# Inverse's last level on one quarter, keys' norms from a diagonal, and four loads moved, in a retention, delta-rule and PEER block

## What is computed

```python
k_g = k_g * lax.rsqrt(jnp.sum(k_g * k_g, axis=-1, keepdims=True) + NORM_EPS)
kkt = jnp.einsum('bhnid,bhnjd->bhnij', kb, k) * lmask      # kb = k * beta
m = jnp.eye(CHUNK) + jnp.where(strict, kkt, 0.0)
sol = lax.linalg.triangular_solve(m, rhs, left_side=True, lower=True, unit_diagonal=True)
...
act = jax.nn.gelu(jnp.einsum('tkd,td->tk', u_tab[ids], xb), approximate=False)
return jnp.einsum('tk,tkd->td', gate * act, v_tab[ids])
```

## Time and profile before

| | before |
|---|---|
| median of 3 runs | 3143.29 us (3141.07 to 3143.57) |
| the profiled execution | 3143.25 us, of which 3141.3 us are the span of its trace |
| busy PE, DVE, ACT, POOL | 76%, 66%, 37%, 37% of the span |
| moved by the DMA engines | 1265.78 MB, mean 403 GB/s |
| of it by the gathers | 1073.81 MB |
| mean granted TensorE clock | 0.878 |

### The profile page before, as it was taken

One profiled execution on the slowest core, in us unless ns is written; L12 is line 12 of the kernel. 1 busy time (PEld: TensorE's weight loads), 2 busy tenths in 40 slices (PEclk: granted clock), 3 DMA queues, 4 the chain that ended last, 5 costly groups with the idle time before them and its releaser, 6 DMA issues.

```text
span 3141.3 us, 36341 instructions
## 1 busy us (share of the span) xinstructions
PE 2386.6 (76%) x12496; PEld 1389.6 (44%) x12496; DVE 2076.6 (66%) x5408; ACT 1173.6 (37%) x3421; POOL 1175.5 (37%) x1030
## 2 busy tenths in 40 slices
PE   8877787998874787997876587798787567765554
PEld 7753355764541345663552144575355124431111
DVE  4475855668579854667749874656856976486444
ACT  2233433344334432435323533424433343232222
POOL 0033533235333442334434443234443444344442
PEclk9998898998987898998998789899998689877777
DMA  8399999999999999999999999999999999999997
GB/s 344 141 405 420 417 411 401 396 409 419 420 415 400 419 420 420 386 418 419 419 420 415 420 419 416 390 405 420 419 420 420 420 419 418 419 402 418 420 420 319
DMA packets 177736, 1265.78 MB, mean 403 GB/s; under 512 B 21520, under 2 KB 21776, under 8 KB 25104
## 3 DMA queue, kind: packets, MB, share of 16 engines
q0 software_dynamic: 147456, 1073.81, 83.0%
q1 hardware_dynamic: 28368, 183.72, 14.2%
q10 hardware_dynamic: 1728, 5.94, 0.5%
HBM read 1259.19 MB, written 4.19 MB: 402 GB/s over the span
## 4 chain that ended last, share of the span: by engine, by line
DMA 36%; PE 36%; DVE 16%; ACT 6%; issue 3%; POOL 3%; SPq 0%; ACTq 0%; POOLq 0%; DVEq 0%
DMA uv<-uv_tab,ids 33%; PE y_ps L476 13%; PE bank L533 8%; DVE uv L1161 7%; PE bank L525 7%; PE bank L540 3%; POOL uv L452 3%; DMA wbuf<-w 2%; ACT diag L847 2%; PE y_ps L555 1%; DVE area L1221 1%; DVE area L1455 1%; PE bank L590 1%; DMA uv<-w 1%; ACT gelu L841 1%
## 5 line engine op out<-in xcount | busy, mean ns | idle before, releaser
L452 POOL DMA_INDIRECT uv<-uv_tab,ids x1024 | 1175.0, 1147 | 1933.0 <-PE y_ps L476 1589.8
L1161 DVE CUSTOM_DVE_ANT_0 uv<-uv,h 128x1024 f32<-128x1024 f32 x1024 | 1237.6, 1223 | 783.9 <-DMA uv<-uv_tab,ids 777.4
L476 PE MATMUL y_ps<-uv,diag 128*64 128x512 f32 x4096 | 1187.2, 712 | 515.2 <-ACT diag L847 494.1
L476 PEld LDWEIGHTS y_ps<-uv,diag 128*64 128x64 f32 x4096 | 289.1, 156 | 1168.5 <-ACT diag L847 687.4
L841 ACT ACTIVATE gelu<-dots 128x2 f32<-128x2 f32 x512 | 104.1, 203 | 1429.8 <-DVE dots L1161 1429.4
L533 PE MATMUL bank<-actT,wbuf 128*128 128x128 f32 x2688 | 343.0, 289 | 42.8 <-DMA wbuf<-w 37.8
L533 PEld LDWEIGHTS bank<-actT,wbuf 128*128 128x128 f32 x2688 | 329.6, 204 | 99.8 <-issue 72.4
L847 ACT ACTIVATE diag<-gated,gelu 128x64 f32<-128x64 f32 x1024 | 300.7, 340 | 66.9 <-PE y_ps L476 8.2
L837 ACT ACTIVATE gated<-smalls,gate 128x64 f32<-128x64 f32 x1024 | 293.9, 336 | 7.8 <-DVE acc L1175 7.8
L525 PE MATMUL bank<-wbuf,actT 128*128 128x256 f32 x960 | 226.8, 390 | 23.3 <-DMA wbuf<-w 21.5
L525 PEld LDWEIGHTS bank<-wbuf,actT 128*128 128x128 f32 x960 | 181.7, 194 | 91.7 <-issue 49.5
(11 more groups left out here) (221 smaller groups left out, 1874.2 us busy)
## 6 DMA issues: line engine op xcount, KB each, us to landing
wbuf<-w SPq DMA_DIRECT2D x146, 1024.0 KB, 9.5
uv<-w SPq DMA_DIRECT2D x20, 1024.0 KB, 23.9
uv<-uv_tab,ids POOLq DMA_INDIRECT x1024, 16.1
acc<-x SPq DMA_DIRECT2D x8, 512.0 KB, 12.8
y<-acc ACTq DMA_DIRECT2D x8, 512.0 KB, 7.6
rowbuf<-x SPq DMA_DIRECT2D x5, 512.0 KB, 12.6
actT_ahead<-x SPq DMA_DIRECT2D x3, 512.0 KB, 19.1
keys_sb<-keysT ACTq DMA_DIRECT2D x1, 1024.0 KB, 16.0
```

What stands on the lines that cost most here:

```text
L452: nc.gpsimd.indirect_dma_start(out=uv[i % RING][:, :, :].rearrange("p z d -> p (z d)"), out_offset=None, in_=uv_tab, in_offset=bass.Indire ...
L476: done = mm(y_ps[z][64 * j:64 * j + 64, :], diag[:, i % DIAGS, :], uv[i % RING][:, 1, 512 * z:512 * z + 512], start=(s % PAIRS == 0), stop ...
L1161: V.tensor_tensor_reduce(out=u, in0=u, in1=h2[n % 2][:, j, :], scale=1.0, scalar=0.0, op0=ALU.mult, op1=ALU.add, accum_out=dots[:, i % DOT ...
```

## The change

Three edits.

1. **Last level.** At level 6 only the lower left 64x64 quarter of P is non-zero after the mask. The change makes that quarter alone for each head (K=64, 64 columns of weights, 64 columns moved), copies it without a mask, leaves Q and the update of `T` out, and makes and subtracts only the upper right quarter of R.
2. **Keys' norms.** `kk` is made from the unscaled keys, before `ss`. DVE multiplies it with the identity and sums along the rows (`tensor_tensor_reduce`, once a head; its product goes to `NT`, which is written again later), which gives the keys' sums of squares in `st[:, 88:92]`; event `kk_sums`. ACT squares q alone, PE's `ss` has 4 matmuls for 8. `beta_row` now scales `cmask` into `kbT`, and `NT` = `kk` times `kbT`. PE's wait for `kbT` is gone; ACT waits for `kk_sums`. The order of the banks changes with it.
3. **Late loads.** The four loads are issued on ACT after the third projection of chunk 0 has been taken in, at the end of its `inputs`.

```diff
-    uses += own(("gc", "gc_in", 1, 0), ("gc_row", "E", 1, 0), ("ss", "norm_in", 1, 0),
-                ("kT", "kst", 1, 0), ("qk", "attn", 1, 0), ("beta_row", "kbT", 1, 0),
-                ("vT", "vb", 1, 0), ("kk", "NT", 1, 0),
+    uses += own(("gc", "gc_in", 1, 0), ("gc_row", "E", 1, 0), ("kk", "NT", 1, 0), ("ss", "norm_in", 1, 0),
+                ("kT", "kst", 1, 0), ("qk", "attn", 1, 0), ("beta_row", "NT", 1, 0),
+                ("vT", "vb", 1, 0),
...
 # PE, mix
+                pe.wait_ge(*event("silu_conv", n, 0))
+                by_head(n, "kk", conv[:, 4:8, :], conv[:, 4:8, :])
                 pe.wait_ge(*event("sq", n))
                 b = take(n, "ss")
-                for i in range(2 * H):
+                for i in range(H):
...
-                pe.wait_ge(*event("kbT", n))
-                by_head(n, "kk", conv[:, 4:8, :], kbT)
...
+                    if i == LEVELS - 1:
+                        b = take(n, f"P{i}")
+                        for h in range(H):
+                            last = mm(b[64:128, P * h:P * h + 64], NT[0:64, h, 64:128], T[0:64, h, 0:64], start=True, stop=True)
+                        given(last)
+                        turn()
+                        pe.wait_ge(*event("inv_P", n, i - 1))
+                        pe.wait_ge(*event("inv_TT", n, i - 1))
+                        b = take(n, f"R{i}")
+                        for h in range(H):
+                            last = mm(b[0:64, P * h + 64:P * h + 128], Pm[64:128, h, 0:64], TT[64:128, h, 64:128],
+                                      start=True, stop=True)
+                        given(last)
+                        turn()
+                        continue
...
 # ACT: the same four act.dma_start(dst, src) leave the place before act.wait_ge(const_in, ...)
                 if c.kind == "start":
+                    for dst, src in ((ret_qdec[:, :, :], qdec), (smalls[:, :], small),
+                                     (keys_sb[:, :, :], keysT), (lnf_row[:, :], rows.partition_broadcast(P))):
+                        act.dma_start(dst, src).then_inc(late_in, 16)
                     return
...
 # ACT, roots and squares
-                    A(st[:, root][:, H:2 * H], b[:, H:2 * H], ACT.Sqrt, bias=eps_col[:, 0:1]).then_inc(S["norm_in"], 1)
+                    act.wait_ge(*event("kk_sums", n))
+                    A(st[:, root][:, H:2 * H], st[:, 88:92], ACT.Sqrt, bias=eps_col[:, 0:1]).then_inc(S["norm_in"], 1)
...
-                A(norms[:, :, :], conv[:, 0:8, :], ACT.Square).then_inc(S["sq"], 1)
+                A(norms[:, 0:4, :], conv[:, 0:4, :], ACT.Square).then_inc(S["sq"], 1)
...
 # DVE, at the end of log_decays
+                    b = filled(dve, "kk", c)
+                    for h in range(H):
+                        last = V.tensor_tensor_reduce(out=NT[:, h, :], in0=b[:, P * h:P * h + P], in1=ident, scale=1.0, scalar=0.0,
+                                                      op0=ALU.mult, op1=ALU.add, accum_out=st[:, 88 + h:89 + h])
+                    last.then_inc(S["kk_sums"], 1)
...
-                V.tensor_tensor(kbT[:, :, :], conv[:, 4:8, :], heads(filled(dve, "beta_row", c)), ALU.mult
-                                ).then_inc(S["kbT"], 1)
+                link(V.tensor_tensor(kbT[:, :, :], cmask[:, :, :], heads(filled(dve, "beta_row", c)), ALU.mult))
...
-                V.tensor_tensor(NT[:, :, :], heads(filled(dve, "kk", c)), cmask[:, :, :], ALU.mult).then_inc(S["NT"], 1)
+                V.tensor_tensor(NT[:, :, :], heads(filled(dve, "kk", c)), kbT[:, :, :], ALU.mult).then_inc(S["NT"], 1)
...
+                i = LEVELS - 1
+                V.tensor_copy(Pm[64:128, :, 0:64], heads(filled(dve, f"P{i}", c))[64:128, :, 0:64]).then_inc(S["inv_P"], 1)
+                turn()
+                corner = TT[0:64, :, 64:128]
+                V.tensor_tensor(corner, corner, heads(filled(dve, f"R{i}", c))[0:64, :, 64:128], ALU.subtract
+                                ).then_inc(S["inv_TT"], 1)
```

More of the change, by code:

```diff
@@ L74, in level @@
             steps = {level + 1: names for level, names in steps.items()}
-        return (own((f"P{i}", "inv_P", LEVELS - 1, i - 1)) + steps.get(i, [])
-                + own((f"Q{i}", "inv_T", LEVELS - 1, i - 1), (f"R{i}", "inv_TT", LEVELS, i)))
+        made = own((f"P{i}", "inv_P", LEVELS - 1, i - 1)) + steps.get(i, [])
+        if i < LEVELS - 1:
+            made += own((f"Q{i}", "inv_T", LEVELS - 2, i - 1))
+        return made + own((f"R{i}", "inv_TT", LEVELS, i))
     both = int(kind == "start")
@@ L295, in build @@
         picked = scores.rearrange("p a (b t) -> p (a b) t", t=TOPK)
-        st = sb("st", [88])
+        st = sb("st", [92])
         rstd2 = st[:, 85:86]
@@ L325, in build @@
             "ret_mixed": 1, "conv_done": 3, "silu_conv": 3, "sq": 1, "beta_k": 1, "sp_in": 1, "exp_ab": 1,
-            "ln_ab": 1, "beta_g": 1, "diff": 1, "exp_diff": 1, "small_exp": 1, "kst_scale": 1, "qd": 1,
+            "ln_ab": 1, "beta_g": 1, "diff": 1, "kk_sums": 1, "exp_diff": 1, "small_exp": 1, "kst_scale": 1, "qd": 1,
             "kbe": 1, "T_init": 1, "gdn_ss": 1, "sqrt_gdn": 1, "mixed": 1, "ss2": 1, "sqrt2": 1, "rstd2": 1,
@@ L912, in inputs @@
                 if n == 0:
-                    for dst, src in ((ret_qdec[:, :, :], qdec), (smalls[:, :], small),
-                                     (keys_sb[:, :, :], keysT), (lnf_row[:, :], rows.partition_broadcast(P))):
-                        act.dma_start(dst, src).then_inc(late_in, 16)
                     act.wait_ge(const_in, 16 * N_CONST)
@@ L1359, in mix @@
                 turn()
-                for i in range(1, LEVELS):
+                for i in range(1, LEVELS - 1):
                     V.tensor_tensor(Pm[:, :, :], heads(filled(dve, f"P{i}", c)), each_head(level_mask[i]), ALU.mult
```

## The result

| | before, beside it | after |
|---|---|---|
| median | 3143.43 us (4 runs, 3141.07 to 3148.46) | 3096.03 us (4 runs, 3095.97 to 3096.13) |
| span of the profiled execution | 3141.3 us | 3094.0 us |
| first gather starts | 136.4 us | 133.05 us |
| mean granted TensorE clock | 0.878 | 0.879 |

The ratio is 0.9847, with a 95% interval of 0.9835 to 0.9859. The kernel became 47.4 us faster, where 2.4 were forecast, and lies far outside the range. The sign was right, the size was not: something acts here that the forecast doesn't have.

What follows compares the result with a forecast made beforehand. It took a serial program, mostly on PE, to bound the kernel up to some 137 us, then the stream's bytes at 420 GB/s. Terms 0.6 + 1.75 = 2.35 us off 3143.25 gave 3140.9 us, range 3136.0 to 3145.5.

Steps and rivals of the forecast that it cites:

- which is this kernel's ceiling: In the stream: most slices move 415 to 420 GB/s, none more, so that was taken as this kernel's highest rate.
- The stream behind it is bound by bytes and shifts as it is: After the first gather: the whole stream was to start and end 2.35 us earlier, otherwise unchanged.
- The bytes are the same in both kernels: Whole traffic, 1265.78 MB: unchanged, so edits were summed on chunk 0's chain, then their effect on the stream was asked.
- The keys' norms: Chunk 0's chain through DVE: 0.6 us gained, bounds 1.4 gained and 2.9 lost; `T` copied at 55.7 us.
- The last level: PE in chunk 0, level 6: P and R at 0.46 us each, saving 1.75 us, bounds 1.5 and 2.2.
- The late loads: ACT in chunk 0: third projection ends 1.4 us earlier, eaten by 2.25 us of issues; keys' SiLU 0.4 us later.
- Late loads too late: Rival at DVE near 58 us: DVE waits for the loads until 65, 6.1 us lost, 3147.0 us; chance 0.07.
- A dry stream in each mix: Rival: the sums ahead of ACT's roots delay the stream in all seven mixes, 9.8 us lost, 3150.7 us; chance 0.05.
- Lulls shrink: Rival after 145 us: PE's lighter mix removes a fifth of the stream's 48 us shortfall, 3131 us; chance 0.13.
- Head start only in part: Rival on chunk 0's chain: only the last level counts, 3141.5 us, or 3144.4 with costlier sums; chance 0.15.
- the case that I held likeliest: Whole kernel: the forecast's own case, 3140.9 us, 3138 to 3143.5 with the lulls' shifts; chance 0.60.

Runs made afterwards that it cites:

- e8: The kernel before with 32 unused bytes ahead of `wbuf`, so weight buffers stay unaligned while gather buffers start at a multiple of 512; 3102.37 us, ratio 0.9879.
- e13: e1 with 32 bytes between `uv4` and `uv5`, so five gather buffers are aligned and five are 32 bytes off; 3117.03 us, ratio 0.9913.
- e2: The changed kernel with the keys' sums in spare columns of `smalls` and `st` at 88 columns, so addresses stay as before; 3141.67 us, ratio 0.9995.
- e1: The kernel before with `st` at 92 columns for 88, nothing else changed, so gather buffers start at a multiple of 512; 3098.35 us, ratio 0.9860.
- e11: e1 plus the quarter-sized last level alone; 3100.69 us, ratio 0.9867.
- e9: e1 plus the move of the four late loads alone; 3101.60 us, ratio 0.9865.
- e14: The changed kernel with the four late loads issued where they were before the change; 3097.69 us, ratio 0.9854.
- e3: The kernel before with `st` at 100 columns, so gather buffers start 32 bytes past a multiple of 512; 3143.20 us, ratio 1.0000.

## Why the prediction was wrong

**The step that failed is "which is this kernel's ceiling"**, and with it "The stream behind it is bound by bytes and shifts as it is". The rows showed a rate that the slices reach and don't pass. I read a rate that was reached as one that nothing in the kernel sets. The stream was bound by its transfers, as I said, but the time of a transfer's packets depended on where they landed: 312.0 ns in the mean for 317.0, 427 GB/s for 420, 45 us. "The bytes are the same in both kernels" was true and beside the point: 1.4% of the time hung on where they land. The diff held the cause in plain sight. The sums go to `st[:, 88:92]`, so `st` grew by 16 bytes, and I costed its instructions and never asked what lies behind it. No rival had a changed packet, so the range couldn't hold the result either.

The trace of before held a hint that I didn't use, packets of one size at 309, 313 and 320 ns. Nothing in my account gave equal packets different times; the question why they had them could have led to their addresses. The Trainium skill, "DMA: Bandwidth & Descriptors", section "How a descriptor splits into AXI transactions", says of reading that a transaction must start at a multiple of 256 bytes, so that the first one of a descriptor which doesn't start there begins at the boundary below, and the bytes before the start are fetched for nothing. An estimate from that, if it held for the landing side too: 33 transactions for 32 at 8 KB, 3%. The runs agree on the step (0 and 256 fast, 32 to 128 and 480 not). They measure 1.6% for the packets' mean (317.0 for 312.0 ns). They don't bear the rule out for an unaligned place by itself (e8, and the first unaligned gathers of e13).

**The parts** came near to what was booked in e2, which has the old addresses, but luck had a share in it. Forecast were 2.35 us for the first gather; it came 1.7 us earlier, and the kernel 1.9. Neither is clear of the spread of equal kernels:

```profile
134.73 1.11 POOL L454 DMA_INDIRECT uv<-uv_tab,ids  x1 [133.50 <-DVE ids L1548]
```

*The keys' norms.* DVE in e2: the first sum, the end of the third convolution, the copy of `T`.

```profile
42.49 0.29 DVE L1267 CUSTOM_DVE_ANT_0 arena<-bank,tab 128x128 f32<-128x128 f32 x1 [3.67 <-PE bank L542]
...
47.77 0.17 DVE L1242 COPY conv_in<-conv_in 128x12 f32<-128x12 f32 x1
...
55.74 0.69 DVE L1380 COPY arena<-bank 128x512 f32<-128x512 f32 x1
```

The convolution ends at 47.9, forecast 47.7, and `T` is copied at 55.74, forecast 55.7, where before had 56.36. So the 0.6 us came out, but by luck: two sizes in it were wrong and nearly cancel. A sum starts every 0.21 us and the four end 0.93 us after the first began, not 1.4; but `kk` before them ended at 42.5, not at 41.7, because the third projection ended only 0.5 us earlier than in before (36.50 for 37.01), not 1.4. The new wait of DVE is there (3.67 us), and it is paid for as booked: the waits for the norms, the exponentials and most of that for `beta_row` are gone. In the changed kernel itself:

```profile
40.78 0.29 DVE L1267 CUSTOM_DVE_ANT_0 arena<-bank,tab 128x128 f32<-128x128 f32 x1
40.99 0.87 DVE L1237 TENSOR_SCALAR area<-conv_in,conv_w 128x128 f32<-128x128 f32 x4
...
45.42 0.17 DVE L1242 COPY conv_in<-conv_in 128x12 f32<-128x12 f32 x1
45.51 0.20 DVE L1281 RECIPROCAL st<-st 128x8 f32<-128x8 f32 x1
...
48.57 0.69 DVE L1292 TENSOR_TENSOR arena<-decayT,bank 128x512 f32<-128x512 f32 x1 [0.75 <-PE bank L547]
...
54.05 0.69 DVE L1380 COPY arena<-bank 128x512 f32<-128x512 f32 x1
```

The ends of the convolution and of `T` lie 2.3 and 1.7 us earlier than in e2, by the same edits. PE shows where that comes from:

```profile
20.53 14.54 PE L535 MATMUL bank<-actT,uv 128*128 128x128 f32 x128
...
38.95 1.16 PE L542 MATMUL bank<-area 128*128 128x128 f32 x8 [2.80 <-ACT area L990]
```

e2 has the third projection at 21.96, with the same length, and `kk` at 40.38. These 1.4 us come from the first projection, whose 64 records took 8.84 us here and 10.31 in e2, with full clock granted in both and no wait shown. e1, aligned, took 9.69, and before, unaligned, 8.99, so I don't put it down to the address. The rest is clock: `kk` took 1.16 us here and 2.08 in e2, because the grant fell near 40 us in both (1.00, the 2.4 GHz level, from 38 to 40 us; 0.50, the 1.2 GHz level, from 42 to 44), and here most of `kk` was through by then.

*The last level.* The chain of waits of the changed kernel:

```profile
88.73 0.60 PE bank L714 x8
89.34 1.92 PE y_ps L557 x8
91.26 0.60 PE bank L721 x8
```

P and R take 0.60 us each where I took 0.46. P, Q and R took 2.67 us before and take 1.20 now, so the saving is 1.47 us for 1.75, a hair outside my bound of 1.5. The term was mis-sized: a quarter costs what the half did, 0.59 us, 75 ns a record. The Trainium skill's "TensorE: Matmul & The Clock Gate" gave 0.23 us by its section on the back-to-back issue gap. The section gives that spacing for a matmul alone and says that it is too low where each has its weight load, as here; the row is 2.6 times 0.23. Alone, on the aligned kernel (e11), the first gather came 0.9 us earlier for 1.47 us saved.

*The late loads.* ACT in the changed kernel:

```profile
35.10 0.60 ACT L886 ACTIVATE conv_in<-bank 128x512 f32<-128x512 f32 x1 [6.55 <-PE bank L535]
35.11 0.38 ACTq L959 DMA_DIRECT2D ret_qdec<-qdec  x1
...
36.49 0.45 ACTq L959 DMA_DIRECT2D lnf_row<-rows  x1
36.97 1.28 ACT L990 ACT_TABLE_LOAD   x1 [1.27 <-issue]
```

The issues begin with the intake, and the table load stands 1.27 us behind its end. That is the mechanism as forecast, with a smaller price: I had 2.25 us of issuing, less 0.5 covered, 1.75. The waits for `uv<-w` at 21 and 26 us are gone, here and in e2. But the third projection, which was to end 1.4 us earlier by that, did so by 0.5 in e2, 1.1 in e9 (35.2 for e1's 36.3) and 2.0 in the changed kernel (35.1 for e14's 37.1). Of these 2.0 the issues leave 0.7 (`kk` at 38.95 for 39.68), and the first gather has nothing of it (133.05 for 133.1): from 40 to 50 us e14 was granted 0.83 of the clock and the changed kernel 0.66. That e9 is 1.7 us late and not level with e1 is mostly its clock. From 40 to 50 us it was granted 0.66, as before was, and its `ss` took

```profile
40.69 3.47 PE L655 MATMUL bank<-tab,area 128*128 128x1 f32 x16 [4.41 <-ACT area L993]
```

where the same 16 records took 2.05 us in e1, granted 0.83 there: 1.4 us.

**The rivals.** *Late loads too late* didn't happen. The slowest landed 16.8 us after its issue at 36.49, at 53.3. From 40 to 50 us ACT's queue and SP's moved as many packets as each other (448 and 445), but SP's were of 8 KB and part of ACT's of 296 bytes to 4 KB, so ACT's had less than half of the bytes. DVE came to the loads later still and found them there, with no wait:

```profile
56.60 0.41 DVE L1320 TENSOR_TENSOR area<-qk_r,ropes 128x256 f32<-128x256 f32 x1
```

*A dry stream in each mix* would have shown as 9.8 us lost in e2, which won 1.9. *Lulls shrink* didn't happen either: 42.2 us before, 44.5 in e2, 44.4 after. *Head start only in part* is what e2 comes closest to, with 1.7 of 2.35 us. At the old addresses the case that I held likeliest would have been right in its number: 3141.7 us measured, 3140.9 forecast. That tests little, since e2 can't be told from no change either (0.9986 to 1.0005).

## What to carry to other kernels

The rate at which this stream of equal transfers levelled off was a limit of the kernel with its present addresses, not of the chip. Before such a rate is called a ceiling, look whether equal packets have equal times. In a diff, every changed size of a buffer is a change to the addresses of all that is allocated behind it. Large buffers that many transfers land in belong at multiples of 256 bytes, put there on purpose, and a change that is meant to save work should be timed once more with the old addresses kept.

## What the runs showed of the hardware

- 8 KB packets into buffers 32, 64, 128 or 224 bytes past a multiple of 256 took 311 to 321 ns, most of them, where aligned ones took 309: in before 420 for 427 GB/s on the saturated engines, 45 us of 3143. It takes a run of unaligned packets: behind aligned gathers the first unaligned one had 90% at 309 ns and the fourth 22% (e13).
- Offsets weren't equal: 32 and 480 past a multiple of 512 gave nothing, 64 and 128 gave 7.5 and 5.7 us, by a lower mean of the packets (313.1 and 312.9 ns within 330 ns, for 314.1).
- Four fp32 products of 64x64 by 64 columns took 0.60 us, as long as with twice the width.
- A multiply-and-sum of 128x128 from PSUM took 0.29 us and started every 0.21; the multiply-and-adds of equal size took 0.35 and started every 0.29 (12 in 3.49 us).
- From 40 to 50 us kernels with equal instructions were granted between 0.51 (e3) and 0.83 (e1) of the clock, and their streams started between 134.4 and 138.4 us, a wider spread than any of the three edits is worth.
